# Turning the softmax weights on VectorE and ScalarE in place of TensorE, with the pair's later steps moved

## What is computed

```python
proj = _rms_norm(x, pre_norm[i]) @ w_in[i]      # -> q | k | v | memory query | gate
q, k = rope(q), rope(k)                          # 12 heads, 2 maps of width 64
scores = einsum('bqhmd,bkhmd->bhmqk', q_blk, k) * 64 ** -0.5   # causal, per block of 128 queries
probs = softmax(scores)
weights = probs[:, :, 0] - lam * probs[:, :, 1]
o = einsum('bhqk,bkhe->bqhe', weights, v)
o = _rms_norm(o, subln_g) * (1 - lambda_init)
branch = concat(o, cross_out) * silu(gate)
x = x + _rms_norm(branch @ w_out[i], post_norm[i])
```

## Time and profile before

| | |
|---|---|
| Median of 3 runs (range) | 963.57 us (959.42 to 963.98) |
| Profiled execution, its own time | 964.46 us |
| Its span, first to last instruction | 962.70 us |
| TensorE matmul busy | 947.7 us, 98% |
| VectorE busy | 630.4 us, 65% |
| ScalarE busy | 475.4 us, 49% |
| DMA, 16 engines | 182 MB, 189 GB/s |
| Mean granted TensorE clock | 0.997 |

### The profile page before, as it was taken

The page is one execution under the profiler, slowest core; times in us unless marked ns, Lnnn a source line. Parts: engine busy times, 40 slices in busy tenths (PEclk is TensorE's granted clock), DMA queues, the critical chain, the costliest instruction groups (busy, mean ns, idle before and its releaser), DMA issues.

```text
span 962.7 us, 14077 instructions
## 1 busy us (share of the span) xinstructions
PE 947.7 (98%) x5148; PEld 813.1 (84%) x5148; DVE 630.4 (65%) x867; ACT 475.4 (49%) x725; POOL 1.2 (0%) x9
## 2 busy tenths in 40 slices
PE   8899999999999999999999999999999999999996
PEld 7788888888888888888888888888888888888885
DVE  5677666656665656645596447457778878886555
ACT  6756634344434343344465445445465465554441
POOL 0000000000000000000000000000000000000000
PEclk9999999999999999999999999999999999999998
DMA  9657555666666656655666655565655765646562
GB/s 330 203 171 260 174 176 178 191 191 192 189 191 181 189 179 191 205 192 194 199 203 201 183 169 179 171 197 167 205 167 162 219 184 164 200 148 203 192 196 89
DMA packets 148762, 182.31 MB, mean 189 GB/s; under 512 B 8112, under 2 KB 116976, under 8 KB 147952
## 3 DMA queue, kind: packets, MB, share of 16 engines
q1 hardware_dynamic: 147776, 177.25, 59.2%
q10 hardware_dynamic: 944, 4.49, 1.2%
HBM read 176.48 MB, written 2.10 MB: 185 GB/s over the span
## 4 chain that ended last, share of the span: by engine, by line
PE 95%; DMA 2%; DVE 1%; ACT 0%; SPq 0%; issue 0%; DVEq 0%; ACTq 0%
PE psum L368 40%; PE psum L369 20%; PE psum L428 10%; PE psum L430 10%; PE psum L429 10%; DMA stage_area<-in_mem_dram 1%; PE psum L604 1%; PE psum L447 1%; PE psum L472 1%; PE psum L455 1%; DMA raw_ring<-in_w_kv_mem_dram 1%; DVE lo_ring L914 1%; PE psum L576 0%; PE psum L464 0%; ACT hi_ring L653 0%; PE psum L586 0%
## 5 line engine op out<-in xcount | busy, mean ns | idle before, releaser
L368 PE MATMUL psum<-hT_split,hi_ring 128*128 128x512 f32 x1600 | 564.4, 398 | 0.0
L914 DVE TENSOR_TENSOR lo_ring<-raw_ring,hi_ring 128x1024 fp32r<-128x1024 f32 x319 | 386.1, 1223 | 256.8 <-ACT hi_ring L653 255.0
L653 ACT ACTIVATE hi_ring<-raw_ring 128x1024 fp32r<-128x1024 f32 x319 | 336.4, 1062 | 398.1 <-PE psum L369 262.0
L369 PE MATMUL psum<-hT_split,lo_ring 128*128 128x256 f32 x1600 | 447.2, 279 | 0.0
L368 PEld LDWEIGHTS psum<-hT_split,hi_ring 128*128 128x128 f32 x1600 | 300.3, 188 | 72.8 <-issue 2.0
L369 PEld LDWEIGHTS psum<-hT_split,lo_ring 128*128 128x128 f32 x1600 | 301.7, 189 | 0.1
L428 PE MATMUL psum<-hi_ring,branchT_split 128*128 128x512 f32 x256 | 99.9, 390 | 0.0
L430 PE MATMUL psum<-hi_ring,branchT_split 128*128 128x512 f32 x256 | 99.6, 389 | 0.0
L429 PE MATMUL psum<-lo_ring,branchT_split 128*128 128x512 f32 x256 | 99.6, 389 | 0.0
L430 PEld LDWEIGHTS psum<-hi_ring,branchT_split 128*128 128x128 f32 x256 | 48.1, 188 | 10.1
L429 PEld LDWEIGHTS psum<-lo_ring,branchT_split 128*128 128x128 f32 x256 | 48.1, 188 | 10.0
(11 more groups left out here) (186 smaller groups left out, 671.8 us busy)
## 6 DMA issues: line engine op xcount, KB each, us to landing
raw_ring<-in_w_in_dram SPq DMA_DIRECT2D x224, 512.0 KB, 4.5
raw_ring<-in_w_out_dram SPq DMA_DIRECT2D x64, 512.0 KB, 4.9
raw_ring<-in_w_kv_mem_dram SPq DMA_DIRECT2D x31, 512.0 KB, 4.6
layer_area<-layer_area SPq DMA_DIRECT2D x48, 64.0 KB, 3.2
stage_area<-in_mem_dram SPq DMA_DIRECT2D x8, 256.0 KB, 7.1
x_residual<-in_x_dram SPq DMA_DIRECT2D x2, 1024.0 KB, 9.7
x_residual<-in_x_dram ACTq DMA_DIRECT2D x1, 2048.0 KB, 10.1
layer_area<-in_post_norm_dram ACTq DMA_DIRECT2D x2, 1024.0 KB, 5.4
```

What stands on the lines that cost most here:

```text
L368: mm(o, hi[:, k, P * c:P * (c + 1)], X[:, kt, :], start=kt == 0, stop=False)
L369: last = mm(o[:, SEQ:], lo[:, k, P * c:P * (c + 1)], X[:, kt, 0:SEQ], start=False, stop=kt == KT - 1)
L653: run(whi[:, slot, :], raw[:, slot, :], ACT.Copy).then_inc(hi_ready, 1)
L914: V_.tensor_tensor(wlo[:, slot, :], raw[:, slot, :], whi[:, slot, :].bitcast(f32), SUB)\
```

## The change

The softmax weights are turned in two steps: VectorE transposes every 32x32 block in one instruction into the second map's half of `prob`, which is free by then, and ScalarE moves the blocks to their places, one copy of 32 partitions x 192 elements for each of 16 pairs of quadrants, eight at key place 1 and eight at key place 2. TensorE's `diff_turn` and ScalarE's `take_weights` are gone. `diff_values` moves from key unit 3 to gate unit 1 and `take_values` with it; `out_norm` moves from key place 3 to gate place 2; `diff_out_turn` moves from gate unit 2 to the next pair's query unit 0, and `out_take` from gate place 2 to the next pair's query place 0. For pair 5 the same steps stand in the first cross gate group's places (0 for pair 4's output) and in the first output row group's (1, 2 and 5). The wait in `diff_scores` is as it was.

```diff
+    prob_blocks = prob[:, :, 1, :]
+    QUADRANTS = [(a, b) for a in range(4) for b in range(4)]
...
-        def diff_turn(p):
-
-            pe.wait_ge(w_ready, p + 1)
-            for h in range(2):
-                for b in range(3):
-                    last = nc.tensor.transpose(ps[:, 4 + h, P * b:P * (b + 1)],
-                                               prob[:, h, 0, P * b:P * (b + 1)], ident)
-            last.then_inc(wt_done, 1)
-
         def diff_values(p):
-            pe.wait_ge(wt_ready, p + 1)
+            pe.wait_ge(wt_ready, p * 16 + 16)
...
-            column_group(G, u, s, XA, at={} if first else {1: lambda: diff_scores(p - 1, second)})
-            column_group(G + 1, u + B_UNITS, 1 - s, XA,
-                         at={} if first else {2: lambda: diff_turn(p - 1), 3: lambda: diff_values(p - 1)})
-            column_group(G + 2, u + 2 * B_UNITS, s, XA, at={} if first else {2: lambda: diff_out_turn(p - 1)})
+            in_query, in_gate = {}, {}
+            if not first:
+                in_query[1] = lambda: diff_scores(p - 1, second)
+                in_gate[1] = lambda: diff_values(p - 1)
+            if not first and not second:
+                in_query[0] = lambda: diff_out_turn(p - 2)
+            column_group(G, u, s, XA, at=in_query)
+            column_group(G + 1, u + B_UNITS, 1 - s, XA)
+            column_group(G + 2, u + 2 * B_UNITS, s, XA, at=in_gate)
...
+        column_group(G_XG1, U_XG1, G_XG1 % 2, XA,
+                     at={0: lambda: diff_out_turn(PAIRS - 2), 1: lambda: diff_scores(PAIRS - 1)})
+        column_group(G_XG1 + 1, U_XG1 + B_UNITS, (G_XG1 + 1) % 2, XA)
...
-                      at={4: lambda: diff_out_turn(PAIRS - 1)} if g == 0 else {},
+                      at={1: lambda: diff_values(PAIRS - 1), 5: lambda: diff_out_turn(PAIRS - 1)} if g == 0 else {},
...
-        def take_weights(p):
-            act.wait_ge(wt_done, p + 1)
-            run(probT, ps[:, 4:6, 0:3 * P], ACT.Copy).then_inc(wt_ready, 1)
+        def move_weights(p, first, last):
+            act.wait_ge(blocks_turned, p + 1)
+            for a, b in QUADRANTS[first:last]:
+                to = probT.rearrange("p h (k a r) -> p h k a r", k=3, a=4)[32 * b:32 * b + 32, :, :, a, :]
+                block = prob_blocks.rearrange("p h (k b r) -> p h k b r", k=3, b=4)[32 * a:32 * a + 32, :, :, b, :]
+                run(to, block, ACT.Copy).then_inc(wt_ready, 1)
...
-                         at={} if first else {2: lambda: take_weights(p - 1), 3: lambda: take_values(p - 1)})
-            column_group(G + 2, u + 2 * B_UNITS, s)
+                         at={} if first else {1: lambda: move_weights(p - 1, 0, 8), 2: lambda: move_weights(p - 1, 8, 16)})
+            column_group(G + 2, u + 2 * B_UNITS, s, at={} if first else {1: lambda: take_values(p - 1)})
...
             last.then_inc(w_ready, 1)
+            dve.wait_ge(w_ready, p + 1)
+            V_.transpose(prob_blocks, prob[:, :, 0, :]).then_inc(blocks_turned, 1)
...
-            in_query, in_keys, in_gate = {}, {}, {0: rope_queries, 3: rope_keys}
+            in_query, in_gate = {}, {0: rope_queries, 3: rope_keys}
             if not first:
                 in_query[1] = lambda: softmax_max(st, p - 1)
                 in_query[2] = lambda: softmax_weights(st, p - 1)
-                in_keys[3] = lambda: out_norm(st, p - 1)
-                in_gate[2] = lambda: out_take(st, p - 1, 1 - parity)
+                in_gate[2] = lambda: out_norm(st, p - 1)
+            if not first and not second:
+                in_query[0] = lambda: out_take(st, p - 2, parity)
...
+                     at={0: lambda: out_take(st, PAIRS - 2, 0), 1: lambda: softmax_max(st, PAIRS - 1),
+                         2: lambda: softmax_weights(st, PAIRS - 1)})
...
-                      at={4: lambda: out_take(st, PAIRS - 1, 1)}
+                      at={2: lambda: out_norm(st, PAIRS - 1), 5: lambda: out_take(st, PAIRS - 1, 1)}
```

More of the change, by code:

```diff
@@ L209, in build @@
     rope_done, s_done, max_ready, exp_done = sem("rope_done"), sem("score_done"), sem("max_ready"), sem("exp_done")
-    w_ready, wt_done, wt_ready = sem("weights_ready"), sem("weights_turned"), sem("weightsT_ready")
+    w_ready, blocks_turned, wt_ready = sem("weights_ready"), sem("weight_blocks_turned"), sem("weightsT_ready")
     pv_done, o_copied, on_ready, n_done, o_taken = sem("pv_done"), sem("o_copied"), sem("o_normed"), sem("o_turned"), sem("o_taken")
@@ L620, in _ @@
             pair(p + 1, (G_PAIR + 1) % 2)
-        column_group(G_XG1, U_XG1, G_XG1 % 2, XA, at={1: lambda: diff_scores(PAIRS - 1)})
-        column_group(G_XG1 + 1, U_XG1 + B_UNITS, (G_XG1 + 1) % 2, XA,
-                     at={2: lambda: diff_turn(PAIRS - 1), 3: lambda: diff_values(PAIRS - 1)})
+        column_group(G_XG1, U_XG1, G_XG1 % 2, XA,
+                     at={0: lambda: diff_out_turn(PAIRS - 2), 1: lambda: diff_scores(PAIRS - 1)})
+        column_group(G_XG1 + 1, U_XG1 + B_UNITS, (G_XG1 + 1) % 2, XA)
         done0 = PAIRS + 1
@@ L897, in _ @@
         column_group(G_XG1 + 1, U_XG1 + B_UNITS, (G_XG1 + 1) % 2,
-                     at={2: lambda: take_weights(PAIRS - 1), 3: lambda: take_values(PAIRS - 1)})
+                     at={1: lambda: move_weights(PAIRS - 1, 0, 8), 2: lambda: move_weights(PAIRS - 1, 8, 16)})
         tanh_of(G_XG1 + 1, val1, tanh1)
         for g in range(4):
-            out_group(4 + g, U_OUT1 + A_UNITS * g, (G_OUT1 + g) % 2, at={1: begin_roots} if g == 1 else {})
+            out_group(4 + g, U_OUT1 + A_UNITS * g, (G_OUT1 + g) % 2,
+                      at={1: begin_roots} if g == 1 else {1: lambda: take_values(PAIRS - 1)} if g == 0 else {})
     @block.vector
@@ L1284, in softmax_weights, with pair @@
             last.then_inc(w_ready, 1)
-        def pair(st, p, s, parity, first=False):
+            dve.wait_ge(w_ready, p + 1)
+            V_.transpose(prob_blocks, prob[:, :, 0, :]).then_inc(blocks_turned, 1)
+        def pair(st, p, s, parity, first=False, second=False):
             G, c, u = p * 3 + G_PAIR, p * 3 + columns_before(G_PAIR, 9), p * (3 * B_UNITS) + U_PAIR
@@ L1297, in pair @@
                 in_query[2] = lambda: softmax_weights(st, p - 1)
-                in_keys[3] = lambda: out_norm(st, p - 1)
-                in_gate[2] = lambda: out_take(st, p - 1, 1 - parity)
+                in_gate[2] = lambda: out_norm(st, p - 1)
+            if not first and not second:
+                in_query[0] = lambda: out_take(st, p - 2, parity)
             column_group(G, c, u, s, two(qT), at=in_query)
-            column_group(G + 1, c + 1, u + B_UNITS, 1 - s, two(kT), at=in_keys)
+            column_group(G + 1, c + 1, u + B_UNITS, 1 - s, two(kT))
             column_group(G + 2, c + 2, u + 2 * B_UNITS, s, val1, at=in_gate)
@@ L1306, in _ @@
         pair(st, 0, G_PAIR % 2, 0, first=True)
+        pair(st, 1, (G_PAIR + 1) % 2, 1, second=True)
         before_pairs, TWO_PAIR_STEPS = st.base + st.n, 2 * (4 + 12 + 1 + 8)
[L1308 to L1311, removed]
+        with dve.Fori(2, PAIRS, 2) as p:
+            st = Steps(dve, dve_step, before_pairs + (p - 2) * (TWO_PAIR_STEPS // 2))
+            pair(st, p, G_PAIR % 2, 0)
+            pair(st, p + 1, (G_PAIR + 1) % 2, 1)
             assert st.n == TWO_PAIR_STEPS, st.n
         st = Steps(dve, dve_step, before_pairs + (PAIRS - 2) * (TWO_PAIR_STEPS // 2))
-        pair(st, PAIRS - 1, (G_PAIR + 1) % 2, 1)
         def cross_branch(i, tanhs):
@@ L1324, in _ @@
         column_group(G_XG1, columns, U_XG1, G_XG1 % 2, val1,
-                     at={1: lambda: softmax_max(st, PAIRS - 1), 2: lambda: softmax_weights(st, PAIRS - 1)})
+                     at={0: lambda: out_take(st, PAIRS - 2, 0), 1: lambda: softmax_max(st, PAIRS - 1),
+                         2: lambda: softmax_weights(st, PAIRS - 1)})
         cross_branch(0, 2 * PAIRS + 3)
-        column_group(G_XG1 + 1, columns + 1, U_XG1 + B_UNITS, (G_XG1 + 1) % 2, val1,
-                     at={3: lambda: out_norm(st, PAIRS - 1)})
+        column_group(G_XG1 + 1, columns + 1, U_XG1 + B_UNITS, (G_XG1 + 1) % 2, val1)
         cross_branch(1, 2 * PAIRS + 4)
```

## The result

The changed kernel takes 986.07 us (median of 4 runs, 982.88 to 991.51) against 963.78 us: ratio 1.0236, interval 1.0208 to 1.0264. A second set of runs gave 986.36 us and 1.0244 (1.0174 to 1.0314). It is slower by some 22.5 us, inside the range forecast and 5.6 us over the figure forecast.

The account below looks back on a forecast made before the run. The prediction took TensorE, busy throughout each pair, as the bound. Its terms, -3.9 (turn) + 19.25 (five waits) + 1.6 (one clock fall) = +16.95 us on the 963.57 us median, gave 980.5 us, range 976.5 to 988.5.

Parts of the forecast that it names:

- TensorE is the bound, and the moved `out_take` decides: In the pairs, TensorE is always busy; it would wait ahead of the scores for VectorE's `out_take`, now later in the queue.
- The wait, five times 3.85 us: Ahead of the scores, TensorE ready at 8.85 us, `o_taken` at 12.6, 0.1 for waking; five times, 19.25 us on.
- The turn saves 3.9 us on TensorE: At key unit 2, removing `diff_turn`'s six transposes takes 0.65 us off each of six pairs, 3.9 us.
- The clock, one fall of 1.6 us: Behind the waits at the scores, one fall to 1.2 GHz was counted, adding 1.6 us; five would be 8 us.
- the 3.2 us of the earlier trace: At the run's end the granted clock fell some 3.2 us after the last matmul; waits of 3.85 us are longer.
- the slow stretch at the run's start: At the run's start, about 3.3 us at the lower clock, half of it, 1.65 us, lost; used as a fall's price.
- the case held likeliest, 0.62 for up to three falls: Five waits of 3.4 to 4.1 us at the scores, up to three clock falls: 976.7 to 985.1 us, chance 0.62.
- The case given 0.22, a fall at every wait: The clock falls at four or five of the waits at the scores: 987.2 us, chance 0.22.
- VectorE's transpose at no cost: Ahead of key unit 2's low part, a 0.9 us transpose costs nothing, nor at 1.8; low part ends 14.5, needed 15.5.
- Values and the last pair at no cost: Moving the six value matmuls to another gap costs nothing; pair 5's branch is ready at 4.4 us, TensorE needs it at 5.9.

Follow-up runs that it names:

- Run 1: The changed kernel with only VectorE's `out_take` moved, to right behind `rope_keys` at gate place 3 of the next pair: 974.53 us, ratio 1.0110.
- run 4: The kernel before with only `diff_out_turn` and `out_take` moved to query place 0 of the pair after the next: 980.10 us, ratio 1.0201.
- run 5: The changed kernel with its new places, but weights turned by TensorE's six transposes and one ScalarE copy, as before: 991.79 us, ratio 1.0310.
- run 3: The changed kernel with `out_take` between `combine` and `silu_twice` at the end of the gate group: 978.68 us, ratio 1.0162.
- run 7: The changed kernel with `out_take` behind `rope_keys` at gate place 3 and `out_norm` at gate place 1: 970.59 us, ratio 1.0087.
- run 8: The changed kernel with `out_take` at gate place 3, `out_norm` at gate place 1, weights turned by TensorE as before: 964.36 us, ratio 1.0019.
- Run 2: The changed kernel with 13 unused matmuls on TensorE ahead of the wait for `o_taken` in `diff_scores`: 978.90 us, ratio 1.0170.

## Why the prediction was right, and where its sizes were off

- **TensorE is the bound, and the moved `out_take` decides**: shown. Run 1 takes the wait away by moving that step only, run 4 makes it by moving that step and the turn of its input.
- **The wait, five times 3.85 us**: 18.3 us in all, 3.66 each. VectorE's chain was right to 0.1 us; the 0.1 us for waking TensorE was right too. TensorE's own path, from gate unit 1's end (720.30) to the end of the last matmul ahead of the wait (729.34), was 9.04 us in place of 8.85. Of the 0.2 us between, 0.07 is only the way of counting: a next matmul starts that much before the end of the last, and the idle time is counted from that end.
- **The turn saves 3.9 us on TensorE**: the accounts of both traces use it and come within 1.5 and 1.2 us, and by run 5 it is 3.3 to 3.6 us. The prices on the other engines were near: the transpose 0.98 us (0.9 said), a copy 0.36 us (0.35 said) with the next starting 0.39 us later. The two groups of the changed kernel (count, then busy us and mean ns of one, then the engine's idle time before them):

```profile
L864 ACT ACTIVATE layer_area<-layer_area 32x192 f32<-32x192 f32 x96 | 34.7, 362 | 2.2
...
L1288 DVE STREAM_TRANSPOSE layer_area<-layer_area 128x768 f32<-128x768 f32 x6 | 5.9, 978 | 0.2
```

The estimate worked out from the Trainium skill ("ScalarE: Activation LUTs", section "What ACT_TABLE_LOAD costs"), about 0.25 us from the start of one copy to the next, is too low here: the measured spacing of 0.39 us decides. It would have changed nothing, as `diff_values` never waited.
- **The clock, one fall of 1.6 us**: this is the term that was mis-sized. There were five falls of 1.4 to 3.0 us, 10.0 to 11.3 us together. Two readings failed. I took the 3.2 us of the earlier trace rows for the shortest pause that counts; runs 3 and 4 show falls behind pauses of 2.1 to 2.6 us, and none behind some others of 2.3 to 2.5. And I took the slow stretch at the run's start as the price of every fall: 1.65 us is right for those of 3.4 us (1.4 to 1.7), but five of the ten last 6.8 us and cost 2.5 to 3.0. So the case held likeliest, 0.62 for up to three falls, did not come. The case given 0.22, a fall at every wait, did, and the time lies in the range because the range took that case in. That its 987.2 us is so near the 986.07 is partly luck: it adds 23.6 us, where the stretch grew by 25.6 to 27.2 and only the medians lie 22.3 apart. The warning of the Trainium skill about long pauses ("TensorE: Matmul & The Clock Gate", section "Why this matters for your kernels") agrees with this case: a fall of the clock went with each of the ten waits of 3.6 to 3.7 us in the two traces.
- **VectorE's transpose at no cost**: right for this kernel, where TensorE waits nowhere but at the scores. Pair 1, which has no such wait, shows that there was room even without it: the low part behind the transpose ended 14.3 us after the scores began (14.5 by the prediction, needed at 15.5). The room goes when `out_take` stands shortly ahead too and the scores no longer wait: then TensorE waits 0.3 to 1.3 us at key unit 2 (runs 1 and 7, 5.3 and 4.9 us in all), and with 0.65 us saved in each pair that is a loss.
- **Values and the last pair at no cost**: right, for the same reason.

In the sum: forecast -3.9 + 19.25 + 1.6 = +16.95, measured in the stretch -3.9 + 18.3 + 11.3 and 1.5 not named = +27.2 (second trace +25.6). The medians show less, +22.3, probably because they mix the two bunches described last.

Of the 1.5 us (1.2 in the second trace) about 1 is TensorE's longer step in the pairs (last section); a few tenths stay open. Open too is what sets whether a pause of 2.1 to 2.6 us is followed by a fall, and whether a fall lasts 3.4 or 6.8 us.

## What to carry to other kernels

Moving a step later in one engine's queue is priced at the wait that it releases, on both sides, counted from one common event: here VectorE's chain of nine steps against TensorE's three units gave the wait to 0.2 us before any run. To a pause of 2.1 us or more of a TensorE that is otherwise always busy, add what the clock may take afterwards: up to 3.1 us here, nearly as much again as the pause. Pauses of up to 1.5 us were followed by none. And work taken off the bound engine is a gain only if the engines that get it have room at that place: VectorE was 80% busy in a pair, and with `out_take` close by, 1 us of transpose cost more than TensorE's 0.65.

## What the runs showed of the hardware that I had not expected

**TensorE's step has two lengths.** One step of the column groups (a 512-column and a 256-column matmul) takes 0.347 or 0.353 us at the same granted clock of 1.00, and keeps its length over hundreds of microseconds. The first and the fifth of five starts in a row, from the mixer loop of the kernel before, and then of the changed one:

```profile
199.74 0.40 PE L368 MATMUL psum<-hT_split,hi_ring 128*128 128x512 f32 x1
...
201.15 0.40 PE L368 MATMUL psum<-hT_split,hi_ring 128*128 128x512 f32 x1
```
```profile
199.82 0.40 PE L370 MATMUL psum<-hT_split,hi_ring 128*128 128x512 f32 x1
...
201.21 0.40 PE L370 MATMUL psum<-hT_split,hi_ring 128*128 128x512 f32 x1
```

Four steps take 1.41 us there and 1.39 here. From the last transpose of cross-attention to the first matmul on its values, the 24 groups of the loop last 271.5 us in one case (113.4 to 384.9) and 266.4 in the other (112.7 to 379.1). All 13 traces have one of these two, seven the longer and six the shorter, whatever the kernel. That is 5.1 us with nothing changed, and fits the two bunches in which the runs of the kernel before fall, 958 to 960.5 and 963.1 to 965.6 us: its two traced runs, 964.46 and 964.03 us, both have the longer loop, and no trace of a run of the lower bunch was had; the arrangement with TensorE's turn, almost its twin, took 960.27 us with the shorter. In the pairs the step changes where small matmuls stand between the units: over the stretch it averages 0.347 us in the kernel before, 0.349 in the changed kernel and in run 8, and 0.350 in runs 1 and 7. There are some 500 such steps, so 0.002 us more is 1 us. What sets it is open.

**The clock falls in shorter pauses than the end of the run suggests**, and a fall lasts 3.4 or 6.8 us and costs between 1.4 and 3.1 us for pauses of the same 3.6 to 3.7 us. Run 2, where TensorE works through most of the pause, has no fall.
